# One late gather of 512 columns, or two of 256, in a mixture of experts that streams its weights

## What is computed

```python
def hier_moe(h, w_rg, b_rg, w_re, b_re, w_gate, w_up, w_down):
    ...
    gates = jnp.sum(jax.nn.one_hot(eid, N_EXPERTS, dtype=F32) * w[..., None], axis=1)
    a = jax.nn.silu(jnp.einsum('nd,edf->nef', x, w_gate)) * jnp.einsum('nd,edf->nef', x, w_up)
    y = jnp.einsum('nef,efd->nd', a * gates[..., None].astype(a.dtype), w_down)
```

## Time and profile before

| | us |
|---|---|
| runs | 1110.72, 1107.67, 1107.58 |
| median | 1107.67 |
| the profiled execution | 1108.89 |
| its span, first to last instruction | 1107.1 |
| TensorE busy | 1048.3 (95%) |
| VectorE busy | 379.1 (34%) |
| ScalarE busy | 255.9 (23%) |

### The profile page before, as it was taken

The page is one execution under the profiler, slowest core; times in us unless marked ns, Lnnn a source line. Parts: engine busy times, 40 slices in busy tenths (PEclk is TensorE's granted clock), DMA queues, the critical chain, the costliest instruction groups (busy, mean ns, idle before and its releaser), DMA issues.

```text
span 1107.1 us, 15627 instructions
## 1 busy us (share of the span) xinstructions
PE 1048.3 (95%) x6160; PEld 582.8 (53%) x6160; DVE 379.1 (34%) x1121; ACT 255.9 (23%) x567; POOL 59.2 (5%) x81
## 2 busy tenths in 40 slices
PE   4699999999999999999989999899899999999986
PEld 3345645577565434444344555556757543444434
DVE  4223014257263223213273300524826322421325
ACT  2130103335232111111142101332523211111114
POOL 1221000001002000000010000000100000000001
PEclk8899999999999999999999999999999999999998
DMA  9976454269809999999992444624660999999991
GB/s 342 355 187 203 164 204 175 77 246 379 280 29 342 403 414 412 413 413 414 412 348 76 152 152 162 229 77 161 224 224 22 378 360 413 412 413 414 413 385 58
DMA packets 92764, 302.67 MB, mean 273 GB/s; under 512 B 5789, under 2 KB 6161, under 8 KB 84369
## 3 DMA queue, kind: packets, MB, share of 16 engines
q1 hardware_dynamic: 88848, 293.83, 69.7%
q0 software_dynamic: 3584, 7.71, 2.8%
q10 hardware_dynamic: 256, 0.09, 0.0%
HBM read 298.41 MB, written 4.99 MB: 274 GB/s over the span
## 4 chain that ended last, share of the span: by engine, by line
PE 86%; DMA 6%; DVE 5%; ACT 1%; issue 1%; SPq 0%; DVEq 0%; ACTq 0%
PE ps L1533 19%; PE ps L1054 18%; PE ps L1064 9%; PE ps L1589 9%; PE ps L1240 8%; PE ps L1355 5%; DMA ring<-in_w_up 4%; PE ps L997 3%; PE ps L1382 2%; PE ps L1384 2%; DMA ring<-in_w_in 1%; PE ps L1328 1%; DMA ring<-in_w_mod 1%; DVE xT L2291 1%; PE ps L1204 1%
## 5 line engine op out<-in xcount | busy, mean ns | idle before, releaser
L1054 PE MATMUL ps<-ring,hT 128*128 128x512 f32 (+1 forms) x480 | 196.6, 567 | 1.3 <-DVE hT L2035 1.3
L1533 PE MATMUL ps<-ring,arena 128*64 128x512 f32 x608 | 172.9, 593 | 5.3 <-DMA ring<-in_w_up 5.3
L1054 PEld LDWEIGHTS ps<-ring,hT 128*128 128x128 f32 x480 | 90.7, 191 | 101.0 <-issue 94.3
L1533 PE MATMUL ps<-slot,arena 128*64 128x512 f32 x352 | 135.8, 593 | 0.0
L2291 DVE SCALAR_TENSOR_TENSOR xT<-ps,modT,xT 128x128 f32<-128x128 f32 (+1 forms) x288 | 97.4, 411 | 64.8 <-PE ps L1240 55.5
L1064 PE MATMUL ps<-hT,ring 128*128 128x384 f32 x320 | 105.5, 488 | 0.0
L1533 PEld LDWEIGHTS ps<-ring,arena 128*64 128x64 f32 x608 | 54.5, 137 | 91.5 <-issue 91.5
L1240 PE MATMUL ps<-mixT,ring 128*128 128x384 f32 x256 | 83.4, 487 | 1.6 <-ACT mixT L1870 1.6
L1064 PEld LDWEIGHTS ps<-hT,ring 128*128 128x128 f32 x320 | 60.1, 190 | 41.9 <-issue 2.1
L2545 DVE TENSOR_TENSOR hT<-ps,arena 128x512 f32<-128x512 f32 x16 | 11.1, 692 | 189.9 <-PE ps L1533 189.9
L1589 PE MATMUL ps<-slot,arena 128*64 128x512 f32 x208 | 72.0, 597 | 0.0
(11 more groups left out here) (381 smaller groups left out, 1231.2 us busy)
## 6 DMA issues: line engine op xcount, KB each, us to landing
ring<-in_w_mod SPq DMA_DIRECT2D x24, 2048.0 KB, 12.4
ring<-in_w_gate SPq DMA_DIRECT2D x38, 1024.0 KB, 12.9
ring<-in_w_up SPq DMA_DIRECT2D x38, 1024.0 KB, 11.6
ring<-in_w_down SPq DMA_DIRECT2D x32, 1024.0 KB, 13.9
ring<-in_w_in SPq DMA_DIRECT2D x14, 2048.0 KB, 12.2
slot<-in_w_down SPq DMA_DIRECT2D x26, 1024.0 KB, 12.9
slot<-in_w_gate SPq DMA_DIRECT2D x22, 1024.0 KB, 12.7
slot<-in_w_up SPq DMA_DIRECT2D x22, 1024.0 KB, 11.6
```

What stands on the lines that cost most here:

```text
L1054: mm = pe.matmul(p[:, 0:n], hT[:, k, t * P:(t + 1) * P], w[:, k, c0:c0 + n], start=(k == 0), stop=(k == KT - 1))
L1533: mm = pe.matmul(out[which][64 * s:64 * s + 64, :], xg[:, k, cols[s]], w[i][:, k % 4, :], start=(k == 0), stop=(k == KT - 1))
```

## The change

One gather of 512 columns, for pairs 4 to 7, stands behind pair 3, in place of one of 256 columns there and one of 256 behind pair 4. Each of its products has 512 columns instead of 256, and there are 48 instead of 96 in a layer. Each group fills one bank with one feature block instead of two halves. The select for columns 256 to 511 moves, in pair 3 on VectorE, from behind the eight gated adds to ahead of them, and TensorE waits for it there. Pair 4 waits for the gather's copies one by one instead of all at once. Since pair 4 is no longer followed by a gather, its scatter blocks 6 and 7 go by the ordinary table (banks 6 and 1 instead of 1 and 5).

```diff
@@ place_products
         if j in GATHER_AFTER:
             part = GATHER_AFTER.index(j)
-            for x in range(8 if part == 0 else 4):
+            for x in range(8):
                 bk.place(("gB", part, x), 6 + x % 2)
...
-GATHER_AFTER = (0, 3, 4)
+GATHER_AFTER = (0, 3)
...
@@ tensor, gate and up products
-                    if j in (4, 6):
-                        for x in range(4):
-                            bk.wait_drained(pe, ("gB", j // 2 - 1, x))
                     for k in range(KT):
...
-                        if j == 1:
-                            bk.wait_drained(pe, ("gB", 0, k))
+                        if j - 1 in GATHER_AFTER:
+                            bk.wait_drained(pe, ("gB", GATHER_AFTER.index(j - 1), k))
...
@@ tensor, the gather
-                        pe.wait_ge(ly.sel_ready, (2, 4, 5)[part])
-                        n = 8 if part == 0 else 4
-                        start = 256 * (part - 1) if part else 0
-                        cols_of = slice(start, start + (384 + JOB_SIZE if part == 0 else 256))
-                        for x in range(n):
+                        pe.wait_ge(ly.sel_ready, (2, 5)[part])
+                        cols_of = slice(0, 384 + JOB_SIZE if part == 0 else 512)
+                        for x in range(KT):
                             p = begin(("gB", part, x))
-                            done(gather(p, [sel_r[:, t, cols_of] for t in range(TILES)],
-                                        [x] if part == 0 else [2 * x, 2 * x + 1]), ("gB", part, x))
+                            done(gather(p, [sel_r[:, t, cols_of] for t in range(TILES)], [x]), ("gB", part, x))
...
@@ scalar, the copies
-                        for x in range(8 if part == 0 else 4):
+                        n = 384 + JOB_SIZE if part == 0 else 512
+                        for x in range(KT):
                             p = full_of(("gB", part, x))
-                            if part == 0:
-                                ins = act.copy(xg[:, x, 0:384 + JOB_SIZE], p[:, 0:384 + JOB_SIZE])
-                            else:
-                                start = 256 * (part - 1)
-                                ins = act.copy(xg[:, 2 * x:2 * x + 2, start:start + 256],
-                                               p[:, :].rearrange("p (k n) -> p k n", k=2))
+                            ins = act.copy(xg[:, x, 0:n], p[:, 0:n])
                             drain(("gB", part, x), ins)
...
@@ vector
+                    if j == 3:
+                        select(sel_r[:, :, 256:512], 12, 4).then_inc(ly.sel_ready, 1)
                     if j == JOB_PAIR:
...
                     for m in range(KT if j > 0 else 0):
                         add_back(j - 1, m)
-                    if j == 3:
-                        select(sel_r[:, :, 256:512], 12, 4).then_inc(ly.sel_ready, 1)
```

## The result

The kernel after takes 1117.34 us (median of 4 executions, 1116.8 to 1119.5) against 1107.62 us before (4 executions, 1105.45 to 1110.72): a ratio of 1.0093 with a 95% interval of 1.0069 to 1.0118. It is slower by 0.9%, some 10 us, where 1110.0 was predicted and the range ended at 1111.5. The profiled execution took 1116.8 us, its span 1115.0. (Of the kernels further down, the one with 36 products had one execution of 4594.58 us at a mean granted clock of 0.22; its ratio leaves that one out.)

What follows compares the result with a forecast made beforehand. Weight loads on the saturated DMA queue were taken to end each layer's expert stage; late loads of 0.9 and 1.4 us sum to +2.3 us, moving the median from 1107.67 to 1110.0 us, range 1107.3 to 1111.5.

Steps and rivals of the forecast that it cites:

- a loss of 0.016 us a product: Late gather behind pair 3: loss at each change of weights, giving 0.229 us a product and 11.0 us in all.
- the row scaled by columns: Upper bound for the late gather: the 416-column row scaled to 512, 0.233 us a product, 11.2 us.
- The rule of the Trainium skill: Rival for the late gather: 216 ns a product, 10.4 us in all, kernel +1.0 us, 1108.7; chance 0.18.
- predicted 0.27: Pair 3: the moved select delays the adds, so the gather starts at 441.28 instead of 441.01, 0.27 us of stall.
- The rival of a full stall: Pair 3: select stalls TensorE by all 1.09 us, slots 6.3 to 6.5 us late, sum 3.9 to 4.5 us; chance 0.12.
- The first hole: Load queue behind pair 3's gather: first down load lands 0.9 us late in layer 0, 1.4 in layer 1.
- The time of a fresh start: A load issued with nearly no cover takes 4.9 us from issue to landing, from earlier rows of 5.0 and 4.8.
- The variant with 4.4 us to landing: First late load by the skill's DMA page, 2.0 us fixed plus bytes: sum 0.45 + 0.9 = 1.4 us.
- so about 2.3 us of cover are needed: Load queue: 5.0 and 4.8 us from issue to landing, of which 2.54 is transfer, so 2.3 us of queued work suffices.
- 3.1 us: above 2.3, no second hole: Next burst with little cover: 7.2 us less 5.5 plus 1.4 leaves 3.1 us, enough, so no further late load.
- The last chunk of pair 7 lands later by the same 0.9 and 1.4 us: End of each layer's expert stage: the saturated queue never makes up a hole, so the last up chunk is equally late.
- TensorE's wait there grows, and the layer ends that much later: Pair 7's last up chunk: waits of 2.41 and 2.85 us grow to 3.6 and 4.6 us, delaying the layer's end.

Runs made afterwards that it cites:

- 36 products: The changed kernel with low parts left out of the late gather for every second feature block; 1111.6 us, ratio 1.0046 to the kernel before.
- the select in two parts: The changed kernel with columns 384 to 511 selected at pair 3's start, only 256 to 383 ahead of the adds; 1115.8 us, ratio 1.0083 to before.
- 24 products: The changed kernel with all low parts left out of the late gather; 1109.5 us, ratio 1.0027 to the kernel before.
- the kernel with 256 columns: The changed kernel with each late gather product of 512 columns made as two of 256, 96 products; 1117.1 us, ratio 1.0099 to before.
- its variant with 24 fewer products: The changed kernel without the late gather's low parts, plus 18 extra transposes ahead of pair 7's middle wait; 1106.5 us, ratio 0.9987 to before.

## Why the prediction was wrong

The mechanism was right: the change spends the queue's cover, the load behind the gather comes late, and a saturated queue never makes it up. Its size was not: +2.3 us predicted, some +10 us measured. By the prediction's own steps, with what the profile after shows:

*The gather.* Predicted 11.0 us from a loss of 0.016 us a product, measured 11.44. With the select in two parts the chain has 11.25 us, 0.234 us a product, but it counts from 0.16 us behind the first product there (438.81 against 438.65 in the timeline); from first product to first down product it is 11.4 us in both. The loss is 0.021 us, and the row scaled by columns, my upper bound of 11.2, was the better guide. The rule of the Trainium skill that the prediction weighed (TensorE: Matmul & The Clock Gate, section Back-to-back issue gap), 216 ns for 512 columns, does not agree with the 234 ns here. The same section of the Trainium skill calls that figure the gap of an isolated product and gives about 131 ns for 512 columns in a stream of weight loads and products, which is further off.

*The select and the stall.* VectorE's timeline:

```profile
435.45 1.09 DVE L2365 TENSOR_TENSOR sel_r<-cst,route 128x256 fp32r<-128x256 f32 x3
436.57 5.29 DVE L2281 SCALAR_TENSOR_TENSOR xT<-ps,modT,xT 128x128 f32<-128x128 f32 x16
```

The select of 1.09 us runs ahead of the adds, as worked out. Behind it the gather is late: its first product starts 4.56 us after its pair's start (438.77 - 434.21) against 441.01 - 436.83 = 4.18 before: 0.4 us of stall, predicted 0.27. The down products start 450.20 - 434.21 = 16.0 instead of 10.1 us after the pair's start: 5.9 us late, predicted 5.5. The rival of a full stall (6.3 to 6.5) didn't come.

*The first hole,* predicted 0.9 and 1.4 us, is 1.8 and 1.7. The cover was 0.6 and 0.7 us, not 1.6 and 1.0: 0.4 us is the lateness above, and in layer 0 the queue ran 0.5 us further ahead than in the profile of before (454.4 - 434.21 = 20.2 us after the pair's start, against 457.6 - 436.83 = 20.8). Counted from before's landing, layer 0 is 1.3 us late. The time of a fresh start, 4.9 us to landing, was exactly as read from the earlier trace rows. This is a term that was mis-sized, worth some 0.8 us in all. (The variant with 4.4 us to landing has a slip: 0.5 us less than 0.9 and 1.4 is 0.4 and 0.9, in all 1.3 us and not 1.4.)

*The step that failed: "so about 2.3 us of cover are needed", and from it "3.1 us: above 2.3, no second hole".* The covers were 3.8 us at the late load of layer 0 and 3.2 at that of layer 1, and the loads landed 4.0 and 4.3 us behind the ones ahead: holes of 1.4 and 1.8 us. I had 2.3 us from loads that start on an idle queue, and it held only for such a load: with 36 products the first load behind the gather had 2.9 us and was on time, while later ones with 4.4 and 6.2 us were 0.7 to 0.8 us late. With 24 products, where no load behind the gather has less than 5.7 us, there is no hole right behind it. I also took a load's landing, which is when the last of its engines is done, as the moment until which the queue is full. The windows speak against that: at 465 to 467 the DMA share is 0.76 and the rate 252 GB/s although the second of the two loads in the row of 457.41 lands only at 467.7. Some of the 16 engines have nothing to do there while others still work, so cover counted by landings is too large. The row of 882 to 892, with 0.85 and 314 GB/s, I had read as a price of missing cover and not as a warning that a thin queue loses in more than one place. That uneven engines are the cause of the second hole fits these rows, but not that of layer 1 with its share of 0.93. In layer 0 there is a rival besides: in the five profiles with one unbroken gather of 48 products of 512 columns, a packet of 16 KB for instructions starts 26.2 to 26.6 us after pair 3's start and the late load lands 4.4 to 4.5 us behind it. With 24 products such a packet stands at 26.7 us as well and no load is late, so it isn't enough by itself; and in layer 1 none stands in the 18 us ahead of the late landing. No run separates these causes, and that of the second hole stays open.

*"The last chunk of pair 7 lands later by the same 0.9 and 1.4 us".* It lands 3.6 and 2.6 us later. In layer 0 that is -0.5 + 1.8 + 1.4 and 0.8 us in three small steps of about 0.3 that I can't place. In layer 1 it is 0.1 + 1.7 + 1.8, some 0.2 of small steps, and -1.1 us: before had a late landing of its own near the end of that layer, which this execution has not.

*"TensorE's wait there grows, and the layer ends that much later": the second step that failed.* The waits there are 3.1 us, but others lie earlier, 0.5 and 1.8 us in layer 0 and 1.7 in layer 1: 5.4 and 4.9 us in all, where 3.6 and 4.6 were predicted. And behind a wait of 3.1 us the granted clock falls to 0.5 for some products, which costs 1.7 and 1.4 us. I had priced a wait at its own length. Before's waits of 2.41 and 2.85 us left the clock at full speed, and I asked nothing about what a longer one would do.

*Sum.* Landing 3.6 + 2.6, clock 1.7 + 1.4: 9.3 us in the two stages, and 0.7 us behind the last pair, 10.0 us, against a difference of medians of 9.7. The sum is of single executions and leaves out the +0.5 us between the layers; what the 0.7 us behind the last pair are is open. In place of the predicted 2.3 us stand 3.1 for the first hole (1.3 and 1.8), 3.2 for the second, -0.1 for the small steps, 3.1 for the clock and 0.7 at the end.

*Of what would show me wrong* I had listed waits in pairs 3 to 5 and a queue without a dip. What came, a second dip and a longer second half of pair 7, was in neither list, though "a short dip there and none later" and "waits of 3.6 and 4.6 us" both turned out wrong.

## What to carry to other kernels

When a kernel's end is set by a saturated load queue, price every edit by the longest stretch in which nothing is given back, not by the work that it adds up to: two gathers of 5.8 us cost nothing and one of 11.4 us cost 10 us, with the same work on TensorE. A queue's cover must be read against stretches in which its landings are evenly spaced; here 5.7 us of it by landings was enough right behind the gather, and with 3 to 4 us in the bursts that followed one load in each layer was 1.4 to 2.0 us late. And a longer wait on TensorE is priced at more than its length once its clock has been seen to fall behind one: look at the granted clock and at the same products at full speed.

## What the runs showed of the hardware

*The clock behind a wait.* In the profiles of the change and its variants, 14 waits of 3.1 to 3.3 us for pair 7's last up chunk stand in an otherwise busy stream. Behind 10 of them the clock fell and the 32 products behind took 8.4 to 10.0 us instead of 7.1; behind 4 (both of the kernel with 256 columns, and layer 0 of two others) it didn't. Behind waits for weights of 2.85 us and less it never fell. It fell elsewhere too: before's last scatter products of layer 0 stand behind waits of 1.64 and 0.48 us for VectorE, and in 566 to 572 us the mean granted clock is 0.72. What decides among the 14 is open.

*Late landings beside a deep queue.* Besides the two holes, fifteen loads with 7 us and more of work ahead of them landed 1.1 to 1.6 us late in the expert stages of the 11 profiles with full loads, three of them in that of before (one at 1065.0, with 16.4 us of cover, 1.1 us late). A packet of 16 KB for instructions starts 2.5 to 4.3 us ahead of each such landing. But most of these packets, some 25 us apart, are followed by no late load; this was only seen side by side, and no run here separates them.

*A gap of 1.9 us with no releaser.* With eighteen more instructions in each pair 7, TensorE stood for 1.9 us in pair 2 of layer 1, in both runs of one kernel, and not in its variant with 24 fewer products. Its cause is open.

*The second hole keeps its place by layer.* In all five profiles with the unbroken gather of 48 wide products the gate load issued 23 us after pair 3's start is 1.4 to 1.5 us late in layer 0, with 3.7 to 3.9 us of cover. In layer 1 the same load with the same cover is at most 0.3 us late, and the up load issued at 29 us, with 3.1 to 3.4 us, is 1.4 to 2.0 us late. Why it comes there, and what its size follows, is open: 36 products gave smaller losses, and 24 none.
